# A decoder layer with 32 experts on one core: a new order of work ahead of the experts, and expert weights in one array by order of use, moved 6, 6 and 4 MB at a time

## What is computed

```python
def _layer(x, s0, buf0, mix_w, ln1_g, ln1_b, moe_w, ln2_g, ln2_b):
    mix, s_new, buf_new = _mixer(x, s0, buf0, *mix_w)
    h = _layer_norm(DEEPNORM_ALPHA * x + mix, ln1_g, ln1_b)
    f = _moe(h.reshape(B * L, D), *moe_w).reshape(B, L, D)
    y = _layer_norm(DEEPNORM_ALPHA * h + f, ln2_g, ln2_b)

    # in _mixer
    h = x @ w_in
    q, k, v, lr, g, u, ga, gb = _split_in(h)
    glog = jax.nn.log_sigmoid((lr @ w_gk2 + b_gk).astype(f32)) / GATE_NORMALIZER

    # in _moe
    logits = (x2 @ w_router).astype(jnp.float32) + b_router.astype(jnp.float32)
    top_v, top_i = lax.top_k(logits, TOP_K)
    gate_w = jax.nn.softmax(top_v, axis=-1)
    def expert_block(args):
        xblk, e = args
        hh = xblk @ w_gu[e] + b_gu[e]
        gate = jnp.minimum(hh[:, :D_FF], SWIGLU_LIMIT)
        up = jnp.clip(hh[:, D_FF:], -SWIGLU_LIMIT, SWIGLU_LIMIT)
        act = (up + 1.0) * (gate * jax.nn.sigmoid(GLU_ALPHA * gate))
        return act @ w_down[e] + b_down[e]
```

## Time and profile before

| | us |
|---|---|
| median of 3 runs | 1251.36 (1251.18 to 1251.57) |
| profiled execution | 1250.48, of which the span 1248.5 |
| TensorE busy | 1161.9 (93% of the span) |
| VectorE, ScalarE, GpSimd busy | 469.7, 254.4, 30.0 |
| moved by DMA | 453.46 MB, mean 363 GB/s |
| 84 transfers of 4 MB, from issue to landing | 30.0 to 31.6 (medians by kind) |

### The profile page before, as it was taken

One profiled execution on the slowest core, in us unless ns is written; L12 is line 12 of the kernel. 1 busy time (PEld: TensorE's weight loads), 2 busy tenths in 40 slices (PEclk: granted clock), 3 DMA queues, 4 the chain that ended last, 5 costly groups with the idle time before them and its releaser, 6 DMA issues.

```text
span 1248.5 us, 15297 instructions
## 1 busy us (share of the span) xinstructions
PE 1161.9 (93%) x6273; PEld 646.2 (52%) x6273; DVE 469.7 (38%) x811; ACT 254.4 (20%) x420; POOL 30.0 (2%) x48
## 2 busy tenths in 40 slices
PE   9999999999999999999898899889988998898995
PEld 7999999988544433433343334324433433343333
DVE  4576665665633231332222222313132323222225
ACT  5553444411201111111110111011111111110113
POOL 0000110200000000000000000000000000000001
PEclk9999999999899999999999999999999999999998
DMA  9636444781699999999999999999999999999994
GB/s 373 226 106 236 164 163 145 249 363 76 244 427 386 434 426 429 433 431 429 435 431 429 433 433 428 434 433 431 430 433 433 428 435 431 429 433 431 429 424 165
DMA packets 25913, 453.46 MB, mean 363 GB/s; under 512 B 3181, under 2 KB 3309, under 8 KB 7816
## 3 DMA queue, kind: packets, MB, share of 16 engines
q1 hardware_dynamic: 21936, 439.62, 83.8%
q0 software_dynamic: 3936, 13.25, 3.2%
HBM read 446.66 MB, written 6.31 MB: 363 GB/s over the span
## 4 chain that ended last, share of the span: by engine, by line
PE 49%; DMA 44%; DVE 4%; ACT 1%; issue 1%; SPq 0%; DVEq 0%; ACTq 0%
DMA ring<-in_w_gu 29%; PE bank L1131 16%; DMA ring<-in_w_down 15%; PE bank L781 12%; PE bank L1157 7%; PE bank L1104 2%; PE bank L827 2%; PE bank L860 1%; PE bank L1181 1%; PE bank L919 1%; PE bank L906 1%; PE bank L1238 1%; PE bank L839 1%; PE bank L909 1%; DVE arena L1831 1%
## 5 line engine op out<-in xcount | busy, mean ns | idle before, releaser
L1131 PE MATMUL bank<-ring,arena 128*64 128x512 f32 x1504 | 336.0, 601 | 31.4 <-DMA ring<-in_w_gu 31.4
L1131 PEld LDWEIGHTS bank<-ring,arena 128*64 128x64 f32 x1504 | 107.7, 138 | 238.0 <-issue 199.0
L1157 PE MATMUL bank<-ring,arena 128*64 128x512 f32 x752 | 172.9, 602 | 24.4 <-DMA ring<-in_w_down 23.2
L781 PE MATMUL bank<-arena_r,ring_r 128*128 128x320 f32 x848 | 183.6, 318 | 0.0
L2104 DVE SCALAR_TENSOR_TENSOR arena_r<-bank,arena,arena_r 64x512 fp32r<-64x512 f32 x62 | 46.5, 750 | 306.8 <-ACT arena_r L1591 306.4
L781 PEld LDWEIGHTS bank<-arena_r,ring_r 128*128 128x128 f32 x848 | 139.9, 189 | 0.6 <-issue 0.4
L1131 PE MATMUL bank<-arena 128*64 128x512 f32 x544 | 120.9, 596 | 6.4 <-DMA arena<-in_w_gu 6.4
L2069 DVE COPY arena<-bank 128x512 f32<-128x512 f32 x32 | 22.1, 692 | 277.8 <-PE bank L1131 277.8
L1157 PEld LDWEIGHTS bank<-ring,arena 128*64 128x64 f32 x752 | 51.8, 138 | 119.4 <-issue 99.6
L1579 ACT ACTIVATE arena<-bank 128x512 f32<-128x512 f32 x32 | 19.1, 598 | 388.5 <-PE bank L1131 388.5
L1692 DVE TENSOR_TENSOR ring_r<-ring,ring_r 128x1024 fp32r<-128x1024 f32 x56 | 67.8, 1222 | 52.9 <-ACT ring_r L1389 52.4
(11 more groups left out here) (300 smaller groups left out, 968.1 us busy)
## 6 DMA issues: line engine op xcount, KB each, us to landing
ring<-in_w_gu SPq DMA_DIRECT2D x42, 4096.0 KB, 30.2
ring<-in_w_down SPq DMA_DIRECT2D x21, 4096.0 KB, 30.0
arena<-in_w_gu SPq DMA_DIRECT2D x14, 4096.0 KB, 31.5
ring<-in_w_mix SPq DMA_DIRECT2D x31, 1024.0 KB, 5.1
arena<-in_w_down SPq DMA_DIRECT2D x7, 4096.0 KB, 31.6
ring<-in_w_gu SPq DMA_DIRECT2D x10, 2048.0 KB, 11.9
arena<-in_w_gu SPq DMA_DIRECT2D x6, 2048.0 KB, 12.5
ring<-in_w_down SPq DMA_DIRECT2D x5, 2048.0 KB, 14.7
```

The source lines that it names most:

```text
L781: last = mm(o[:, 0:NT], w[a][:, 1, c, :] if n == 0 and a == 1 else w[a][:, c, f0:f0 + 128], rhs[b][:, c, :], start=c == 0 and a + b == 0, ...
L1131: last = mm(ex[i][side * CAP:(side + 1) * CAP, :], xgt[:, 2 * j + c, block * CAP:(block + 1) * CAP], w[:, c, i * D + side * 512:i * D + (s ...
L1157: last = mm(ex[4][side * CAP:(side + 1) * CAP, :], actt[:, 4 * j + c, :], w[:, c, side * 512:(side + 1) * 512], start=j == 0 and c == 0, s ...
```

## The change

**Ahead of the experts.** x comes in four pieces and the first half of unit 0 in two, in turn. Two matmuls on zeros are left of six. k0 is formed in plain fp32 from the raw pieces, 8 matmuls; k1 takes the form that k0 had. For lr, w_lr's high and low halves lie side by side in the columns (`wlr_both`), so that 16 matmuls do what 24 did; lr then has 32 rows, and w_gk2 is loaded twice. q1 stands between gk1 and gk2. The first gather now forms rows, one-hot by h, 512 columns at a time (`rows_part`, `last_rows`); ScalarE and VectorE copy a half each out of PSUM, TensorE transposes (`turn_rows`), and ScalarE copies to `xgt`. Eight matmuls whose result nobody reads (`keep_warm`) stand around the last ranks. Some semaphores are merged.

**The expert weights.** Units 18 to 27 come one by one, and so do 180 to 185. Units 28 to 179 lie in one new array, `w_groups`, group behind group: 2 units where the number leaves 2 by 8, 3 units where it leaves 4 or 7. A group of 3 is one transfer of 6 MB with rows of 48 KB, one of 2 is 4 MB with rows of 32 KB. SP waits until the unit eight below the group's last one has been used, and a group lands under one semaphore.

```diff
+GROUPS = [(n, {2: 2, 4: 3, 7: 3}[n % 8]) for n in range(FIRST_GROUP, GROUPS_END) if n % 8 in (2, 4, 7)]
...
-            for i in range(2):
-                sp.dma_start(x_raw[:, 4 * i:4 * i + 4, :],
-                             x_t[:, 4 * i * NT:4 * (i + 1) * NT].rearrange("p (c t) -> p c t", t=NT)).then_inc(x_in[i], 16)
+            for i in range(4):
+                sp.dma_start(x_raw[:, 2 * i:2 * i + 2, :],
+                             x_t[:, 2 * i * NT:2 * (i + 1) * NT].rearrange("p (c t) -> p c t", t=NT)).then_inc(x_in[i], 16)
+                if i < 2:
+                    sp.dma_start(ring[:, 0, 512 * i:512 * (i + 1)], w_mix[0, :, 512 * i:512 * (i + 1)])\
+                        .then_inc(raw_in[i], 16)
...
+            def next_group(n, size, m=None):
+
+                wait_used(n + size - 1 - SLOTS, m)
+                first = n - FIRST_GROUP
+                load_group(first if m is None else m * (PERIOD * EXP_UNITS) + first, size, place(n))
...
-            for _ in range(6):
+            for _ in range(2):
                 mm(ps[7][:, :], v[:, 0, 0:128], v[:, 0, 0:512], start=True, stop=True)
             o = claim(("k", 0))
+            raw = parts(0)[0]
+            for c in range(KC):
+                if c % 4 == 0:
+                    pe.wait_ge(raw_in[c // 4], 16)
+                if c % 2 == 0:
+                    pe.wait_ge(x_in[c // 2], 16)
+                last = mm(o[:, 0:NT], raw[:, 0, c, :], x_raw[:, c, :], start=c == 0, stop=c == KC - 1)
...
             for c in range(KC):
-                for a, b in THREE:
-                    last = mm(o[:, 0:NT], wlr_parts[a][:, c, :], xt[b][:, c, :],
-                              start=c == 0 and a + b == 0, stop=c == KC - 1 and a == 1)
+                for b in range(2):
+                    last = mm(o[:, 0:NT], wlr_both[:, c, :], xt[b][:, c, :], start=c == 0 and b == 0,
+                              stop=c == KC - 1 and b == 1)
...
+            def rows_part(i):
+
+                t, a, half = ORDER[i // 4], i // 2 % 2, i % 2
+                mm(ex[(6, 5)[half]][:, :], onehot[:, 0, t, :], h_parts[a][t][:, half * 512:(half + 1) * 512],
+                   start=i < 2, stop=False, skip_group_check=True)
+
+            def last_rows(half):
+
+                mm(ex[(6, 5)[half]][:, :], oh1, hrow[:, 1, half * 512:(half + 1) * 512], start=False, stop=True,
+                   skip_group_check=True).then_inc(gathered, 1)
+
+            def keep_warm(count):
+
+                for _ in range(count):
+                    mm(ex[7][:, :], ident_r, h_parts[0][0][:, 0:512], start=True, stop=True)
+
+            def turn_rows(half):
+
+                pe.wait_ge(rows_kept[half], 1)
+                for c in range(4):
+                    last = nc.tensor.transpose(ex[2 + half][:, c * 128:(c + 1) * 128], xg_rows[:, 4 * half + c, :], ident)
+                last.then_inc(rows_turned, 1)
...
-            last_gather(0)
+            last_rows(0)
             pe.wait_ge(h_ready, 6)
-            last_gather(1)
+            last_rows(1)
+            released(2)
+            turn_rows(0)
+            released(3)
+            turn_rows(1)
```

More of the change, by code:

```diff
@@ L454, in build @@
         gathered = sem("gathered")
+        rows_kept = [sem(f"rows_kept{i}") for i in range(2)]
+        rows_turned = sem("rows_turned")
         xgt_ready = sem("xgt_ready")
@@ L549, in build @@
         FILLS = list(MIX_FILLS)
+        GROUP_OF = {n: g for g, size in GROUPS for n in range(g, g + size)}
         LANDED = {}
@@ L553, in build @@
                 continue
-            in_pair = FIRST_PAIR <= n <= LAST_PAIR + 1
-            s = POSITIONS[place(n - n % 2 if in_pair else n)]
-            if not (in_pair and n % 2):
+            s = POSITIONS[place(GROUP_OF.get(n, n))]
+            if GROUP_OF.get(n, n) == n:
                 FILLS[s] += 1
@@ L653, in _ @@
                 load_unit(*unit_at(n), place(n))
[L654 removed]
+            for n in range(SLOTS + 1, FIRST_GROUP):
                 next_unit(n)
[L656 removed]
+            with sp.Fori(0, GROUP_LOOPS) as loop:
                 m = sp.snap(loop)
[L658 to L662 removed]
+                for n, size in GROUPS:
+                    if n < FIRST_GROUP + PERIOD * EXP_UNITS:
+                        next_group(n, size, m)
+            for n, size in GROUPS:
+                if n >= FIRST_GROUP + GROUP_LOOPS * PERIOD * EXP_UNITS:
+                    next_group(n, size)
+            for n in range(GROUPS_END, NE * EXP_UNITS - 2):
                 next_unit(n)
@@ L818, in _ @@
                     .then_inc(full(("gk", i))[0], 1)
-            for i in range(1, 4):
+                if i == 1:
+                    weights_times("q", 1, xt)
+            for i in range(2, 4):
                 weights_times("q", i, xt)
@@ L2330, in laid_out @@
     a["w_last"] = a["w_down"][NE - 1, 0].reshape(128, KC, 2, 512).swapaxes(1, 2).reshape(128, PAIR)
+    w_groups = np.empty((GROUPS_END - FIRST_GROUP, 128 * 2 * UNIT), np.float32)
+    for first, size in GROUPS:
+        rows = []
+        for n in range(first, first + size):
+            is_up, e, j = unit_at(n)
+            rows.append(a["w_gu" if is_up else "w_down"][e, j // 2, :, j % 2 * 2 * UNIT:(j % 2 + 1) * 2 * UNIT])
+        w_groups[first - FIRST_GROUP:first - FIRST_GROUP + size] = np.concatenate(rows, axis=1).reshape(size, -1)
+    a["w_groups"] = w_groups
     c_cols, a["starts"], a["lists"] = constants()
```

184 lines of the change are left out of this document (84 added, 100 removed).

## The result

The changed kernel takes 1253.96 (median of 19 runs, 1252.52 to 1256.22) where the kernel before takes 1251.18 in the same series (19 runs, 1248.70 to 1252.14): a ratio of 1.0027, 95% interval 1.0020 to 1.0034. By the medians it is slower by 2.8, by the ratio 3.4, more than the 2.5 that the prediction took as the least that can be told from no change. The forecast was 1251.0 and "the same"; the time lies inside the range of 1247.0 to 1255.2, but the change was forecast at 0.35 less and came out as more.

What follows compares the result with a forecast made beforehand. TensorE bounds the first stage, the DMA queue the weight stream; -6.05 (head) + 4.6 (gap) - 2.0 (rows) + 3.1 (end) = -0.35 from 1250.48 gives 1250.1, or 1251.0 as median; range 1247.0 to 1255.2.

Steps and rivals of the forecast that it cites:

- What bounds the kernel: TensorE's matmuls up to about 325 us, then the DMA queue at 432 GB/s; a first-stage gain moves the stream forward.
- Start: First matmuls: k2 starts at 15.5 instead of 16.44, and lr is shorter; a gain of 2.0.
- The 1.2 of lr: Part of the start: the lr product drops from 24 to 16 matmuls, a gain of 1.2.
- gk: With q1 between the gk products, the clock drop behind them was expected not to come; a gain of 1.75.
- 0 if it comes anyway: Lower bound of the gk gain: nothing gained if the clock drop behind the gk products still comes.
- Gather: First gather before unit 0: matmuls moved off the path and eight warming matmuls holding the clock; a gain of 2.3.
- rival 1: At the gather: the clock falls all the same, 2.3 gained becomes 1.3 lost, 1254.6; chance 0.17.
- Gap: Stream's start: the queue runs dry before the first group, units 28 to 30; a loss of 4.6, ends 3.9 to 5.0.
- Wide rows: Units 28 to 177: fewer, wider DMA rows at up to 20 ns a row; a gain of 2.0, at most 3.0.
- Rival 2: In the stream: wide rows do nothing, it stays at 432 GB/s and the time is 1253.0; chance 0.12.
- End: Last experts: groups land whole, so TensorE reaches unit 184 later after the same landing; a loss of 3.1.
- the head: Everything up to the end of unit 0: start, gk and gather together were to gain 6.05.

Runs made afterwards that it cites:

- head_only: Changed start, gk order and gather, with the weight stream of the kernel before (pairs for units 18 to 185): 1248.00 against 1250.25 for the kernel before, ratio 0.9979.
- x_halves: Changed kernel with x in two halves and the first half of unit 0 in one transfer: 1252.64 against 1250.25 for the kernel before, ratio 1.0017.
- rows_16k: Changed kernel with each group moved as separate 2 MB transfers with 16 KB rows: 1260.79 against 1250.25 for the kernel before, ratio 1.0078.
- gk_row: Changed kernel with the four gk products in a row again, keeping 32 rows: 1253.87 against 1250.25 for the kernel before, ratio 1.0030.
- end_172: Changed kernel with groups only up to unit 171, units 172 to 189 one by one: 1249.53 against 1250.25 for the kernel before, ratio 0.9995.

## Why the prediction was wrong, step by step

- **What bounds the kernel** was right: two stages, a lead of the first carried through the second (head_only), and the cut of the stream as the question.
- **Start: the step that failed.** 2.0 gained was booked, 0.4 was lost (lr ended at 27.38 instead of 27.03). The 1.2 of lr came as worked out. The other part rested on transfers landing as in the earlier trace rows, and the delay by four more issues and narrower rows was bounded at 0.4. The transfers were 2.1 to 2.3 late, and k2 with them. SP alone takes some 0.43 for each of the four issues, 1.7 in all, and I had given the rows of 16 KB a price from the earlier trace rows without asking the same of rows an eighth as wide, which are on the path there. The split between issues and rows is open; x_halves takes back the rows and three of the issues, and starts k2 at 15.82, where 15.5 was forecast.
- **gk: a term that rested on one execution.** 1.75 booked, 1.2 between the two profiles, and this because the clock fell in the profiled execution of before; it doesn't in two others, and against those the new order costs 0.4. The bound "0 if it comes anyway" asked about after; the open side was before.
- **Gather:** 2.3 booked, 1.8 measured between the two profiles (unit 0's end led by 2.6, 0.8 of it from the start and gk). The eight matmuls held the clock, which was the step with the doubt; rival 1 did not come. Here too the old head varies: unit 0 behind it takes 4.45, 3.80 or 3.65.
- **Gap:** 4.6 booked with 3.9 to 5.0, 5.5 measured. Mechanism, place and order of size right: issue at 428.70 (431.0 less 2.3 of the lead of 2.6), landing 18.9 behind it where I had 18.4.
- **Wide rows:** 2.0 booked, 1.5 to 2.3 measured; rows_16k shows the slope from the other side. Rival 2 falls: transfers of 2 MB on 128 partitions ran at 427.6 GB/s where those of 6, 6 and 4 MB ran at 432.5. The Trainium skill (DMA: Bandwidth & Descriptors, Rules for kernel authors) asks for 1 MiB and 128 partitions, by which both would be at full bandwidth; these runs differ from it by 1.1%. The Trainium skill's ceiling of 435.2 GB/s (same page, Where 436 GB/s comes from) agrees with the traces: no mean over 100 us between 400 and 1100 us reads above 435 in any run.
- **End:** 3.1 booked, 4.3 measured in this execution; 2.6 of it is the burst of three units, 1.7 the low clock of the first of them. gk_row took its unit there at full clock and reached unit 184 at 1201.66, 41.6 behind that landing, so the 1.7 does not come in every execution. end_172 shows the place, but takes the burst and the low clock away together.

By size: the head came out 3.4 short, gap and end 2.1 dearer, rows 0.3 better; 5.2 in all, from -0.35 to 4.8 in the profiled execution. The medians are 2.8 apart because the profiled execution of before lay 0.7 below its median and that of after 1.3 above its own, the latter with the 1.7 in it.

## What to carry to other kernels

In this kernel a wide transfer costs at its two ends: it waits for all its slots, and it lands whole. Cut small where the queue would run dry or where the consumer has no slack left, wide between; here that, with the start and gk changed back in part, turned 3.4 lost into 10.1 gained. Most of this comes from the small cuts (7.1 and 4.0 above): the wide rows themselves are worth 1.5 to 2.3, and pairs with the same small cuts were not run. And before a gain is booked on a clock that the trace shows low, see whether a second execution shows it too.

## What was not expected of the hardware

- The granted clock fell or held at the same place in the same code: behind gk 12.32 or 10.78 for the same 72 matmuls, in the gather 1.96 or 3.16.
- Behind waits of 2.3 to 2.9 us in the stream, the first unit takes 3.65 in some cases and 5.35 in others. Where TensorE has slack this cost nothing seen; at the end it cost 1.7.
- At the start, with four pieces of x and two of unit 0 in rows of 2.5 and 2 KB, the queue moved 247 GB/s from 5 to 6 us, where it moved 322 with rows of 5 and 4 KB (x in halves) and 420 (before, in another order). Fewer issues may have a part in it.
